# One way or another of turning the attention outputs: TensorE transposes into PSUM, or VectorE block transposes with a round trip through device memory

## What is computed

```python
def diff_attn_block(q, k, v, ..., lam, lam_init, subln_g):
    s = einsum('bqhcd,bkhd->bchqk', ...) * DQK_ATT ** -0.5 + bias     # masked
    p = softmax(s)
    w = p[:, 0] - lam * p[:, 1]
    o = einsum('bhqk,bkhd->bqhd', w, v)
    return rms_norm(o, subln_g) * (1.0 - lam_init)    # over DV = 256

mix = concatenate([att (4 heads x 256), hm (4 heads x 256)])
x = x + mix @ w_out
```

## Time and profile before

| | |
|---|---|
| median of 3 runs | 1754.01 us (1753.78 to 1754.36) |
| profiled execution | 1757.45 us |
| its span | 1755.6 us |
| TensorE, matmuls busy | 1744.9 us |
| TensorE, weight loads busy | 1582.7 us |
| VectorE busy | 898.7 us |
| ScalarE busy | 669.1 us |
| GpSimd busy | 207.1 us |
| granted clock of TensorE | 1.00 in each stretch |
| attention stage | about 240 to 451 us of the span |
| heads' stage and output projection | about 451 to 620 us |

### The profile page before, as it was taken

How to read it: one execution, slowest core, us unless ns; L and a number is a source line. 1 busy time by engine, 2 the same in 40 slices (tenths; PEclk the granted TensorE clock), 3 DMA queues, 4 the chain that set the end, 5 groups by cost and what they waited for, 6 DMA issues and landing times.

```text
span 1755.6 us, 27160 instructions
## 1 busy us (share of the span) xinstructions
PE 1744.9 (99%) x9270; PEld 1582.7 (90%) x9270; DVE 898.7 (51%) x1718; ACT 669.1 (38%) x1256; POOL 207.1 (12%) x286
## 2 busy tenths in 40 slices
PE   9999999999999999999999999999999999999999
PEld 7999998899997789999888999888999888999887
DVE  5634776666677645454344454344444334545333
ACT  5323754444354444333332333333333333333332
POOL 3301010002352210110000110000111000111000
PEclk9999999999999999999999999999999999999999
DMA  7675469998798554444344444334443434444442
GB/s 182 189 181 149 122 163 222 197 202 217 198 258 261 152 142 115 125 121 130 121 131 120 128 122 123 129 124 127 121 130 120 131 120 130 121 122 129 141 147 96
DMA packets 381393, 261.54 MB, mean 149 GB/s; under 512 B 92444, under 2 KB 328156, under 8 KB 381324
## 3 DMA queue, kind: packets, MB, share of 16 engines
q1 hardware_dynamic: 353190, 222.09, 45.1%
q0 software_dynamic: 13072, 34.68, 7.6%
q10 hardware_dynamic: 15062, 3.86, 1.1%
HBM read 244.90 MB, written 21.46 MB: 152 GB/s over the span
## 4 chain that ended last, share of the span: by engine, by line
PE 96%; DVE 2%; SPq 1%; DMA 1%; issue 0%; ACT 0%; ACTq 0%; DVEq 0%
PE acc L520 18%; PE acc L521 18%; PE acc L522 17%; PE bank L607 8%; PE bank L608 8%; PE bank L606 8%; PE bank L1895 3%; PE ssb L606 2%; PE ssb L607 2%; PE ssb L608 2%; PE ssb L1895 1%; PE bank L566 1%; PE bank L567 1%; PE bank L565 1%; SPq L874 1%; PE acc L565 1%
## 5 line engine op out<-in xcount | busy, mean ns | idle before, releaser
L500 DVE TENSOR_TENSOR w_lo<-raw,w_hi 128x512 fp32r<-128x512 f32 x768 | 556.6, 733 | 780.5 <-ACT w_hi L491 779.9
L491 ACT ACTIVATE w_hi<-raw 128x512 fp32r<-128x512 f32 x768 | 482.2, 630 | 830.4 <-PE acc L522 402.6
L521 PE MATMUL acc<-x2g_lo,w_hi 128*128 128x384 f32 x1024 | 348.0, 340 | 0.0
L520 PE MATMUL acc<-x2g_hi,w_hi 128*128 128x384 f32 x1024 | 345.8, 338 | 0.0
L522 PE MATMUL acc<-x2g_hi,w_lo 128*128 128x384 f32 x1024 | 344.6, 337 | 0.0
L520 PE MATMUL acc<-a_hi,w_hi 128*128 128x400 f32 (+1 forms) x768 | 268.1, 349 | 0.2 <-DVE w_lo L500 0.2
L521 PE MATMUL acc<-a_lo,w_hi 128*128 128x400 f32 (+1 forms) x768 | 262.9, 342 | 0.0
L522 PE MATMUL acc<-a_hi,w_lo 128*128 128x400 f32 (+1 forms) x768 | 262.3, 342 | 0.0
L607 PE MATMUL bank<-w_lo,a_hi 128*128 128x512 f32 x640 | 253.0, 395 | 0.0
L608 PE MATMUL bank<-w_hi,a_lo 128*128 128x512 f32 x640 | 252.6, 395 | 0.0
L606 PE MATMUL bank<-w_hi,a_hi 128*128 128x512 f32 x640 | 252.0, 394 | 0.0
(11 more groups left out here) (339 smaller groups left out, 1517.0 us busy)
## 6 DMA issues: line engine op xcount, KB each, us to landing
raw<-in_w_up SPq DMA_DIRECT2D x128, 512.0 KB, 4.0
raw<-in_w_down SPq DMA_DIRECT2D x128, 512.0 KB, 3.7
raw<-in_w_in SPq DMA_DIRECT2D x94, 512.0 KB, 4.6
raw<-in_w_out SPq DMA_DIRECT2D x32, 512.0 KB, 4.6
vc<-in_cache_v POOLq DMA_DIRECT2D x32, 256.0 KB, 6.8
kc<-in_cache_k SPq DMA_DIRECT2D x128, 64.0 KB, 3.1
state_blocks<-in_state_C POOLq DMA_DIRECT2D x16, 256.0 KB, 4.5
C_blk<-state_blocks SPq DMA_DIRECT2D x4, 1024.0 KB, 8.9
```

The lines of the kernel that those rows point to most:

```text
L491: e.activation(w_hi[:, q], raw[:, slot, 4 * (q % 2):4 * (q % 2) + 4, :], ACT.Copy).then_inc(hi_ready, 1)
L500: e.tensor_tensor(w_lo[:, q], raw[:, slot, 4 * (q % 2):4 * (q % 2) + 4, :], w_hi[:, q].bitcast(F32), ALU.subtract).then_inc(lo_ready, 1)
L520: e.matmul(out, w_hi[:, q, kk], hi[:, k, at], start=k == 0, stop=False, skip_group_check=True)
L521: e.matmul(out, w_hi[:, q, kk], lo[:, k, at], start=False, stop=False, skip_group_check=True)
```

## The change

The two TensorE transposes and the two ScalarE copies of each step go. Instead VectorE's `transpose` turns each 32x32 block of `o_rows` in place within its block, into a new buffer `o_blk` (two of them). Four DMAs on ScalarE's queue, one for each 32 rows, write it to a new array `att_out` in device memory, laid out by feature (8 x 128 rows) and token (384 columns), in pieces of 32 numbers (16 for a stream step). Their task, ostore, stands one slot after oturn (the last one in the same slot, 71). GpSimd loads all of it back into `zt` once both buffers' stores have landed and TensorE has read the last queries, ahead of `load_C(0)`. The factor g_sub moves into att_mix: a scale of ScalarE's copy, and a scalar_tensor_tensor in place of VectorE's subtraction.

```diff
-STEP_AT = (..., ("oroot", 5), ("oturn", 7))
+STEP_AT = (..., ("oroot", 5), ("oturn", 7), ("ostore", 8))
...
-        elif what == "oturn":
-            u.add(("oT", STEPS[n]), 1)
...
+        att_out = nc.dram_tensor("att_out", [8 * P, 3 * P], F32).ap()
+            o_blk = sb("o_blk", [P, 2, 8, 32], scope=s)
...
@@ gpsimd, after done(e, ("o", STEPS[-1])) and the wait for v_stored
+            for x in range(2):
+                e.wait_ge(S(f"o_stored{x}"), 16 * 4 * 8)
+            done(e, ("s", STEPS[-1], 1))
+            dma(zt[:, 0:8, LIVE], att_out.rearrange("(k p) t -> p k t", p=P), "att_back")
...
@@ scalar
                     elif what == "osum":
                         o = take(e, ("o", step))
                         if n >= 2:
-                            done(e, ("oT", STEPS[n - 2]))
+                            e.wait_ge(S("o_turned"), n - 1)
...
-                    elif what == "oturn":
-                        b = take(e, ("oT", step))
-                        for half in range(2):
-                            ... e.activation(zt[...], ..., ACT.Copy, scale=g_sub[:, half:half + 1])
-                        taken(ins, ("oT", step))
+                    elif what == "ostore":
+                        e.wait_ge(S("o_turned"), n + 1)
+                        for a in range(4):
+                            rows = slice(32 * a, 32 * a + 32)
+                            if is_stream(step):
+                                at, width = a * 2 * P * 3 * P + 2 * P + step * TD, TD
                             else:
                                 _, h, i = step
+                                at, width = h * 2 * P * 3 * P + i * P + 32 * a, 32
+                            e.dma_start(bass.AP(tensor=att_out.tensor, offset=at,
+                                                ap=[[3 * P, 32], [32 * 3 * P, 8], [1, width]]),
+                                        o_blk[rows, n % 2, :, 0:width]).then_inc(S(f"o_stored{n % 2}"), 16)
...
                     elif what == "att_mix":
-                        read_out(e, *[("oT", a) for a in STEPS])
+                        e.wait_ge(S("att_back"), 16)
                         for k in range(4 * h, 4 * h + 4):
-                            e.activation(a_hi[:, k, LIVE], zt[:, k, LIVE], ACT.Copy)...
+                            e.activation(a_hi[:, k, LIVE], zt[:, k, LIVE], ACT.Copy,
+                                         scale=g_sub[:, k % 2:k % 2 + 1])...
@@ vector
+                    elif what == "oturn":
+                        read_out(e, ("o", STEPS[n]))
+                        if n >= 2:
+                            e.wait_ge(S(f"o_stored{n % 2}"), 16 * 4 * (n // 2))
+                        e.transpose(o_blk[:, n % 2].rearrange("p c t -> p (c t)"),
+                                    o_rows[:, n % 2]).then_inc(S("o_turned"), 1)
...
-                            tt(a_lo[:, k, LIVE], zt[:, k, LIVE], a_hi[:, k, LIVE].bitcast(F32),
-                               ALU.subtract)...
+                            stt(a_lo[:, k, LIVE], zt[:, k, LIVE], g_sub[:, k % 2:k % 2 + 1],
+                                a_hi[:, k, LIVE].bitcast(F32), ALU.mult, ALU.subtract)...
@@ tensor
-            def turn_out(n, b):
-                read_out(e, ("o", b))
-                turn(("oT", b), [(half * P, o_rows[:, n % 2, half * P:(half + 1) * P]) for half in range(2)])
...
-                    elif what == "oturn":
-                        turn_out(n, STEPS[n])
```

More of the change, by code:

```diff
@@ L118 @@
 BLOCKS_AT = (-4, -3, -2, -1)
-STEP_AT = (("scores", 0), ("exp", 0), ("weights", 0), ("turn", 3), ("out", 4), ("osum", 4), ("oroot", 5), ("oturn", 7))
+STEP_AT = (("scores", 0), ("exp", 0), ("weights", 0), ("turn", 3), ("out", 4), ("osum", 4), ("oroot", 5), ("oturn", 7), ("ostore", 8))
 OUT_STEPS = ("osum", "oroot", "oturn")
@@ L1042, in att_work @@
                     yield slot
-                    step = STEPS[n] if what in ("exp", "turn", *OUT_STEPS) else None
+                    step = STEPS[n] if what in ("exp", "turn", "ostore", *OUT_STEPS) else None
                     if what == "ko_store":
@@ L1085, in att_work @@
                         taken(e.activation(o_rows[:, n % 2], o[:, 0:DV], ACT.Copy, scale=c[:, 5:6]), ("o", step))
-                    elif what == "oturn":
-                        b = take(e, ("oT", step))
-                        for half in range(2):
-                            bh = b[:, half * P:(half + 1) * P]
+                    elif what == "ostore":
+                        e.wait_ge(S("o_turned"), n + 1)
+                        for a in range(4):
+                            rows = slice(32 * a, 32 * a + 32)
                             if is_stream(step):
[L1091 to L1094, removed]
+                                at, width = a * 2 * P * 3 * P + 2 * P + step * TD, TD
                             else:
                                 _, h, i = step
-                                at = META + i * P
-                                ins = e.activation(zt[:, 2 * h + half, at:at + P], bh, ACT.Copy,
-                                                   scale=g_sub[:, half:half + 1])
-                        taken(ins, ("oT", step))
+                                at, width = h * 2 * P * 3 * P + i * P + 32 * a, 32
+                            e.dma_start(bass.AP(tensor=att_out.tensor, offset=at,
+                                                ap=[[3 * P, 32], [32 * 3 * P, 8], [1, width]]),
+                                        o_blk[rows, n % 2, :, 0:width]).then_inc(S(f"o_stored{n % 2}"), 16)
             side = Side(att_work())
@@ L1162, in head_work @@
                         e.wait_ge(w_used, 4 * (T_OUT - 1) + h + 1)
-                        read_out(e, *[("oT", a) for a in STEPS])
+                        e.wait_ge(S("att_back"), 16)
                         for k in range(4 * h, 4 * h + 4):
-                            e.activation(a_hi[:, k, LIVE], zt[:, k, LIVE], ACT.Copy).then_inc(S("mix_hi_made"), 1)
+                            e.activation(a_hi[:, k, LIVE], zt[:, k, LIVE], ACT.Copy,
+                                         scale=g_sub[:, k % 2:k % 2 + 1]).then_inc(S("mix_hi_made"), 1)
             side = Side(head_work())
@@ L1743, in head_work @@
                             e.wait_ge(S("mix_hi_made"), k + 1)
-                            tt(a_lo[:, k, LIVE], zt[:, k, LIVE], a_hi[:, k, LIVE].bitcast(F32),
-                               ALU.subtract).then_inc(S("mix_lo_made"), 1)
+                            stt(a_lo[:, k, LIVE], zt[:, k, LIVE], g_sub[:, k % 2:k % 2 + 1],
+                                a_hi[:, k, LIVE].bitcast(F32), ALU.mult, ALU.subtract).then_inc(S("mix_lo_made"), 1)
                     elif what == "rows":
```

## The result

The changed kernel takes 1756.42 us (median of 22 runs, 1755.23 to 1758.06), the kernel before 1753.98 us beside it (22 runs, 1753.48 to 1755.2). The ratio is 1.0013, 95% interval 1.0007 to 1.0019: 2.4 us slower, where 4.1 us faster was forecast. That lies inside the 0.2% that I had called no change, but the interval excludes a gain. The profiled execution took 1756.67 us with a span of 1754.7, so this one stands 0.25 us above its median, where the one of before stood 3.4 above.

What follows compares the result with a forecast made beforehand. TensorE's stream was taken to bound the kernel. Transposes -3.52, first wait -1.14 and load back +0.6 gave -4.06 us: 1754.0 - 4.1 = 1749.9 us, range 1748.3 to 1758.

Steps and rivals of the forecast that it cites:

- The transposes on TensorE: Attention steps: two 128x128 transposes fewer in each of 16 steps, 0.22 us of the chain per pair, 3.5 us gained.
- The first wait: TensorE's 2.1 us stop at 273.64 us for scaled rows goes; 1.1 us gained, the rest waiting for turned weights.
- VectorE's blocks: One 128x256 block transpose per step, 446 ns, 7.1 us of VectorE in all, hidden by ready weight quarters: costs nothing.
- ScalarE's queue: Four issues per step ahead of osum, 1.4 us; osum 0 to 0.7 us late against 2.0 us of cover: nothing.
- Held stores: Rival: ScalarE's four issues ahead of osum are held, 1.21 us each; 9 us slower, 1763 us; chance 0.13.
- DMA engines and small pieces: 1024 pieces per step at 13.4 ns, 0.86 us, cost nothing; rival at 40 ns: late weights, 6 us slower, chance 0.07.
- The load back: 1.5 MB load ahead of head 0's state load; state lands at 468 to 475 us, 0.6 us lost, bounds 0 and 4.

Runs made afterwards that it cites:

- stores_in_wait: Changed kernel with each step's four store issues moved from ahead of osum into ScalarE's wait at the next step's oroot: 1754.23 us, ratio 1.0001 to the kernel before.
- few_pieces: Changed kernel without the load back, each of a step's four store issues writing 32 pieces in place of 256: 1754.28 us, ratio 1.0001 to the kernel before.

## Why the prediction was wrong

**The transposes on TensorE: right.** 3.5 us from the chain's 0.22 us for a pair, which was read at one place; 3.2 measured, and TensorE's distance behind the key blocks shrank by 0.22 to 0.25 us a step.

**The first wait: wrong, 1.1 us too much.** It is not in the second execution of before, and the changed kernel has no wait of about 1 us for the turned weights near 276, which was to be left of it. An execution 3.4 us above its own median had something that the others had not, and I priced it as if every run had it.

**VectorE's blocks: right by themselves.** 434 ns each (446 expected), and no time when they come alone. The reason given was too coarse, though: the ready weight quarters cover the splits, not the key block that stands behind the output block in its slot. The scalar_tensor_tensor takes 610 ns (608 expected).

**ScalarE's queue: the step that failed.** I wrote "2.0 us of cover against 0.7: nothing". Both numbers miss. Four issues took 1.8 to 2.4 us in most steps and not 1.4, since one close behind another takes 0.47 to 0.49 us, and the key store of the first half stands ahead of them; so osum comes 1.03, 1.43 and 1.43 us late ahead of the first three stops, above my 0 to 0.7. And the cover was taken at the one reader that I followed, the turned weights. Another stands on VectorE: osum, the mean, the scores, the weights, the turned keys and the last key block follow each other in its queue, and that block's reader on TensorE had 0.5 to 1.2 us. The two parts that were right to cost nothing by themselves spent it: TensorE's pair (0.22 to 0.25) and VectorE's block (0.24 to 0.33). The lateness of osum then falls on the path. Up to 340 us, where key stores are issued too and the margins were least, TensorE stops for 0.94, 1.42 and 0.97 us; after that for 0.31 and 0.32, and for 0.16 and 0.17 at the two steps whose blocks had 0.5 us more. (In that second half osum is 0.85 to 1.15 us late, and more of it is taken back by the margin or on the way.) Before, 0.5 us of margin stood against 0.24 + 0.24 + 1.03 at the first stop; that is the sum which the prediction should have made, at the last key block.

**Held stores, the rival on the slow side.** Its sign came true and its place was named (the four issues ahead of osum), but not its mechanism: it asked for 0.85 us an issue and for late turned weights, in some 10 steps. The median was 0.47, TensorE waited for a bank (the scores), and 0.47 was enough because the true margin was smaller. Single issues did reach 1.6 us. No wait of TensorE for turned weights stands in the trace of the change; they came when the stores or the blocks had been moved (2.0 us in stores_in_wait). The price of 0.31 us an issue, at most 0.41, was read from 275 to 345 us alone; some 12 us ahead of it the same key stores had reached 1.48.

**DMA engines and small pieces: right in that the engines cost nothing.** Neither the 13.4 ns packets nor the rule of the Trainium skill (DMA: Bandwidth & Descriptors, "Specifications") on transfers under 512 bytes shows in the time: with the stores on GpSimd's queue the kernel is within 0.2 us of the one without stores. On ScalarE's queue 1.7 us went with the pieces (few_pieces), which stays open. Another section of that page, "Issuing engines are not separate DMA queues", has it that issuing from several engines saves no more than the sequencer's issue time. The runs agree as far as they go: the move from ScalarE's queue to GpSimd's left the DMA share as it was (1.07 and 1.06) and took 5.5 us away. Here that issue time, ahead of ScalarE's osum, is most of the change's cost.

**The load back: right in its mechanism.** VectorE waits 2.06 us and TensorE doesn't, as the 3.75 us of room had it. The 0.6 us in the sum has no stop of TensorE to show for it; the runs give 0.5, not told from nothing. (The range of 468 to 475 for the landing is about 1.1 us above what its own terms add up to, 456.9 + 9.9 and 456.9 + 17; no source is given for the difference.)

The sum by what the runs show: -3.2 + 0 + 5.2 + 0.5 = +2.5 us, against 2.4 measured. These terms are the differences from one kernel to the next, so they must add up to the whole and prove nothing; what supports the account is that each stands by its own trace, 4.0 of the 5.2 us as TensorE's stops.

## What to carry to other kernels

Several edits that each cost nothing may draw on the same margin: for each reader on the path, sum what all of them take from it. For work added to an engine's queue, that means every reader behind it, through the other engines' queues too, and not only the one that the moved work used to serve. A DMA issue is not free because its bytes are: give it to a queue that nobody waits for, even where each issue is longer there. And compare the profiled execution with the median of the runs first; a stall in one that lies well above it may not be there to be won.

## What the runs showed of the hardware

- ScalarE's DMA issue took 0.31 us alone and 0.47 to 0.49 us in a row, and up to 1.61 us. Its median hardly depends on the pieces: 474 to 476 ns with 256, 444 ns with 32.
- A key store, 0.31 us at the median, took up to 1.48 and 1.51 us in the two traces of the kernel before.
- The same DMA took 585 ns to issue on GpSimd (584 to 619), steadier and longer.
- In stores_in_wait key stores issued 1.6 and 1.4 us after four others had ended took 2.08 and 3.14 us in place of 0.31, with the DMA share at 1.10 and 1.06.
- 32x32 transposes on VectorE took 434 ns for 128x256 in fp32; a pair of 128x128 transposes in fp32 within TensorE's stream cost 0.2 us (3.2 us / 16), where the record of each one lasts 272 ns.
